# Gated attention's levels without the products of constants between them

## The reference

```python
def hybrid_layer(x, ...):
    proj = (rms_norm(x, pre_gain) * (1.0 + scale) + shift) @ w_in
    a_out = sliding_window_attention(aq, ak, av, sinks) * silu(ag)
    r_out = rms_norm(retention(rq, rk, rv)) * silu(rg)
    log_a = log_sigmoid(ga @ gla_gate_w + gla_gate_b) / 16.0
    g_out = rms_norm(gated_linear_attention(gq, gk, gv, log_a), gla_norm_gain) * silu(gg)
    y = concatenate([a_out, r_out, g_out]) @ w_out
    return x + gate * rms_norm(y, post_gain)

def gated_linear_attention(q, k, v, log_a):   # 4 heads, chunks of 64 tokens
    def step(state, inp):
        b = cumsum(gi, axis=2)
        rel = b[:, :, :, None, :] - b[:, :, None, :, :]
        decay = where(causal, exp(minimum(rel, 0.0)), 0.0)
        sc = einsum('bhid,bhijd,bhjd->bhij', qi, decay, ki)
        intra = einsum('bhij,bhjv->bhiv', sc, vi)
        inter = einsum('bhid,bhdv->bhiv', qi * exp(b), state)
        new_state = exp(b_last) * state + einsum('bhjd,bhjv->bhdv', ki * exp(b_last - b), vi)
        return new_state, intra + inter
```

## Time and profile before

| | |
|---|---|
| median of 3 runs | 2572.66 us (2561.11 to 2583.42) |
| profiled execution | 2573.33 us, its span 2571.6 us |
| mean granted TensorE clock | 0.962 |
| PE busy | 2359.1 us (92%) |
| DVE, POOL, ACT busy | 1318.0 (51%), 1064.4 (41%), 854.2 us (33%) |
| L245, all products of constants | 312 instructions, 78.2 us busy |

### The profile page before, as it was taken

One profiled execution on the slowest core, in us unless ns is written; L12 is line 12 of the kernel. 1 busy time (PEld: TensorE's weight loads), 2 busy tenths in 40 slices (PEclk: granted clock), 3 DMA queues, 4 the chain that ended last, 5 costly groups with the idle time before them and its releaser, 6 DMA issues.

```text
span 2571.6 us, 33845 instructions
## 1 busy us (share of the span) xinstructions
PE 2359.1 (92%) x13354; PEld 1980.2 (77%) x13354; DVE 1318.0 (51%) x2026; ACT 854.2 (33%) x1637; POOL 1064.4 (41%) x799
## 2 busy tenths in 40 slices
PE   4998898987989889888999999999798999999998
PEld 4777787776878656667998989999687677788886
DVE  6785636976559555477523513223678772110113
ACT  2124133224241666643221212112322883322222
POOL 4343346324362332323642433433652343645455
PEclk9998799989998999998999999999999999999999
DMA  8550024420224200023232313232261001223332
GB/s 283 174 165 1 19 81 148 147 83 1 75 70 146 54 2 1 9 79 127 82 99 86 110 58 115 82 95 94 78 196 43 8 2 49 82 92 98 98 99 74
DMA packets 147734, 218.99 MB, mean 85 GB/s; under 512 B 18484, under 2 KB 71124, under 8 KB 147448
## 3 DMA queue, kind: packets, MB, share of 16 engines
q1 hardware_dynamic: 147576, 216.82, 26.7%
HBM read 214.69 MB, written 2.10 MB: 84 GB/s over the span
## 4 chain that ended last, share of the span: by engine, by line
PE 55%; DVE 4%; ACT 3%; issue 2%; POOL 1%; ACTq 0%; DMA 0%; DVEq 0%; POOLq 0%; SPq 0%
PE ps L307 14%; PE ps L308 14%; PE ps L309 14%; PE ps L1008 5%; PE ps L1036 3%; PE ps L1058 2%; DVE mod_acc_aux L367 1%; PE ps L1305 1%; PE ps L1055 1%; POOL h_transposed L580 1%; PE ps L394 1%; PE ps L1300 1%; DVE x_tokens L867 1%; PE ps L592 0%; ACT att_probs_two L1098 0%
## 5 line engine op out<-in xcount | busy, mean ns | idle before, releaser
L296 POOL TENSOR_TENSOR w_lo<-w_raw,w_hi 128x1024 fp32r<-128x1024 f32 (+3 forms) x252 | 589.5, 2340 | 1002.6 <-ACT w_hi L289 1002.5
L289 ACT ACTIVATE w_hi<-w_raw 128x1024 fp32r<-128x1024 f32 (+3 forms) x252 | 255.7, 1016 | 1162.6 <-PE ps L309 981.1
L307 PE MATMUL ps<-w_hi,h_transposed 128*128 128x512 f32 (+3 forms) x1088 | 419.0, 385 | 57.2 <-POOL w_lo L296 30.7
L308 PE MATMUL ps<-w_lo,h_transposed 128*128 128x512 f32 (+3 forms) x1088 | 409.6, 376 | 0.0
L309 PE MATMUL ps<-w_hi,h_transposed 128*128 128x512 f32 (+3 forms) x1088 | 409.4, 376 | 0.0
L307 PE MATMUL ps<-h_transposed,w_hi 128*128 128x384 f32 (+1 forms) x1056 | 374.6, 355 | 8.3 <-POOL h_transposed L580 6.7
L308 PE MATMUL ps<-h_transposed,w_hi 128*128 128x384 f32 (+1 forms) x1056 | 373.9, 354 | 0.0
L309 PE MATMUL ps<-h_transposed,w_lo 128*128 128x384 f32 (+1 forms) x1056 | 373.8, 354 | 0.0
L367 DVE SCALAR_TENSOR_TENSOR mod_acc_aux<-w_raw,c_act,mod_acc_aux 128x512 f32<-128x512 f32 x280 | 279.1, 1021 | 45.0 <-DMA w_raw<-in_w_mod_dram 20.1
L307 PEld LDWEIGHTS ps<-w_hi,h_transposed 128*128 128x128 f32 x1088 | 214.4, 197 | 102.7 <-POOL w_lo L296 35.5
L1500 DVE TENSOR_TENSOR ffn_full<-ps,ffn_silu 128x768 f32<-128x768 f32 (+1 forms) x44 | 34.2, 819 | 427.5 <-PE ps L309 427.5
(11 more groups left out here) (318 smaller groups left out, 3527.5 us busy)
## 6 DMA issues: line engine op xcount, KB each, us to landing
w_raw<-in_ada_w_dram SPq DMA_DIRECT2D x96, 512.0 KB, 3.9
w_raw<-in_ffn_w_in_dram SPq DMA_DIRECT2D x88, 512.0 KB, 3.6
w_raw<-in_w_mod_dram SPq DMA_DIRECT2D x48, 512.0 KB, 4.6
w_raw<-in_ffn_w_out_dram SPq DMA_DIRECT2D x44, 512.0 KB, 3.5
w_raw<-in_w_in_dram SPq DMA_DIRECT2D x40, 512.0 KB, 4.5
w_raw<-in_w_out_dram SPq DMA_DIRECT2D x16, 512.0 KB, 4.3
w_raw<-in_od_w_in_dram SPq DMA_DIRECT2D x16, 512.0 KB, 4.3
mod_gain<-in_norm_g_dram SPq DMA_DIRECT2D x16, 256.0 KB, 4.3
```

The lines of the kernel that those rows point to most:

```text
L289: act.activation(w_hi[:, i % 2, 0:k * n], w_raw[:, u % 4, 0:k * n], ACT.Copy).then_inc(w_hi_ready.sem, 1)
L296: pool.tensor_tensor(w_lo[:, i % 2, 0:k * n], w_raw[:, u % 4, 0:k * n], w_hi[:, i % 2, 0:k * n].bitcast(F32), ALU.subtract).then_inc(w_lo_ ...
L307: pe.matmul(acc, left[0], right[0], start=start, stop=False)
L308: pe.matmul(acc, left[0], right[1], start=False, stop=False)
```

## The change

In `Memories.tensor` the products of constants before level 0 and between and behind the levels are taken out: 5 + 1 + 2 + 5 + 8 = 21 in each of the two layers, 42 in all. The 16 at the phase's end stay, as do those of other phases. Nothing else is changed; no wait and no signal hangs on the products.

```diff
                 self.retained(pe, 3)
-                keep_clock(pe, 5)
                 for l in range(len(LEVELS)):
                     self.level_scores(pe, l)
                     if l == 0:
...
                         self.retention_out(pe, 0)
-                        keep_clock(pe, 1)
                     if l == 1:
...
                     if l == 3:
                         self.retention_out(pe, 3)
-                        keep_clock(pe, 2)
-                    if l >= 4:
-                        keep_clock(pe, 5 if l == 4 else 8)
                 for t in range(XT):
                     self.gated_out(pe, t)
                 keep_clock(pe, 16)
```

## The result

The changed kernel took 2591.6 us (median of 9 runs, 2583.9 to 2597.0) and the kernel before, in the same jobs, 2573.2 us (9 runs). The ratio is 1.0077, with a 95% interval of 1.0053 to 1.0101: 0.8% slower, 0.4 us from the forecast of 2592 and within 1% as the likeliest case had it. The profiled execution has a span of 2589.8 us, 18.2 more than that of before, and a mean granted clock of 0.946 against 0.962. One of the twelve runs of experiment 5 (2786.9 us, mean clock 0.808) and one of experiment 6 (3864.1 us, 0.556) fell in a slow state at a low clock and are left out of what follows.

A forecast was written before the change was run, and what follows sets the result against it. TensorE at low clock bounds the levels, DVE from level 3's end to level 5's placing, TensorE the phase's end. First layer +5.25 and second +14.15 make +19.4 us on 2573.3: forecast 2592 us (chance 0.50), range 2571 to 2606.

The forecast's parts named there:

- The five before level 0, cost 0: Products before level 0: removal gives no time; a slower level 0 (1.99 for 1.13 us) hides in the 7.0 us gap.
- The product after the first output, 2.1 us gained: Single product ahead of level 1, on the path: removal saves 1.1 us in the first layer, 1.0 in the second.
- The second layer's levels at the low clock, +8.8 us: Without the product before level 1, the second layer's levels stay at low clock like the first's: +8.8 us, bounds 0 and 8.8.
- The outputs at the low clock, +5.1 us a layer: Four gated outputs after level 5 start at low clock and take 11.5 instead of 6.4 us; bounds 0 and 5.1.
- Rival 1: Clock returns by itself, in the gated outputs or the second layer's levels: +11.7 or +10.6 us, 2583 to 2585; chance 0.20.
- The closing sixteen, +1.25 us a layer: Sixteen products at the phase's end, on the path, spend 2.5 us at low clock, half lost; bounds 0.5 and 6.5.
- The late products, no time given back: Products after levels 3, 4 and 5 lie beside DVE's placing, so removing them gains 0.
- DVE's chain unchanged: DVE's steps from level 3's placing to level 5's stay at 12.6 us; a sign to check in the changed profile.
- Rival 2: Products are ballast; real work raises the clock after the first output: 2571 us, or 2562 if both layers rise; chance 0.10.
- rival 3: Low clock lasts through the closing sixteen, or next phase's transposes start low: 2 x 5.3 us more, 2603; chance 0.10.
- rival 4: Nothing seen, because before is often in the low case too and the later products' part is regained: 2576 to 2582; chance 0.10.
- the three times of before: 2561, 2573 and 2583 us could be both layers' levels at full clock, one, and none.

The follow-up runs named there:

- experiment 5: Kernel before without the five products ahead of level 0, in both layers: 2578.7 us, ratio 1.0014 to before.
- experiment 6: Kernel before with fourteen products in the wait behind level 0, without the one after the first output and the fifteen after levels 3 to 5: 2572.0 us, ratio 0.9996.
- experiment 1: Kernel before without the one product after the first retention output, in both layers: 2581.5 us, ratio 1.0008 to before.
- experiment 7: Changed kernel also without the closing sixteen products, so none in the phase: 2589.2 us, ratio 1.0061 to before.
- experiment 2: Kernel before without the fifteen products after levels 3, 4 and 5, in both layers: 2587.8 us, ratio 1.0047 to before.
- experiment 3: Kernel before with three products in place of the one after the first retention output: 2563.3 us, ratio 0.9948 to before.
- experiment 4: Kernel before with fourteen products in TensorE's wait behind level 0 and without the one after the first output: 2554.2 us, ratio 0.9908 to before.
- experiment 10: The kernel of experiment 4 run again, on the same chip as experiment 9: 2558.7 us, ratio 0.9934 to before.
- experiment 8: Kernel before with eight products before level 0, thirteen behind it, none after the first output, six instead of eight after level 5: 2558.1 us, ratio 0.9948.
- experiment 9: Kernel before with eight products before level 0, thirteen behind it, none after the first output, late ones unchanged: 2557.8 us, ratio 0.9937 to before.

## Why the prediction was right

**The five before level 0, cost 0:** right. The changed kernel's level 0 took 1.99 us, and experiment 5 shows the gap hiding it.

**The product after the first output, 2.1 us gained:** from the transposes' start to level 1's the layers took 3.47 and 3.46 us in place of 4.43 and 4.36, 1.9 us in all.

**The second layer's levels at the low clock, +8.8 us:** 31.34 - 22.66 = 8.7 us. That products in this place raise the clock, and not where the phase falls alone, is shown by the profiled layers: up before level 2 in none of six without one (changed kernel, experiments 1 and 7), in two of six with one (before and experiments 2 and 5), and in both with three (experiment 3). But the place counts as well, and one product failed more often than it worked.

**The outputs at the low clock, +5.1 us a layer:** 329.21 - 317.54 = 11.7 and 692.29 - 680.61 = 11.7 us against 6.4, so +5.3. Experiments 2 and 6 show it with levels 1 to 3 at the full clock in a layer. Rival 1, by which the outputs raise it themselves, fell: 0.50 over all 11.6 us.

**The closing sixteen, +1.25 us a layer:** 8.35 and 9.41 against 7.13 us, +1.2 and +2.3. The first is right; the second rose 4.6 us in (the sixteen begin at 692.29) and not 2.5. This term was too small in the second layer and in experiment 6 (+2.4 and +1.9). The price of 0.85 us for a product at the low clock was read from a pair in which the clock rose; it stands all the same, since a pair wholly at the low clock takes 2.02 us (experiment 1) and a single one 1.17.

**The late products, no time given back:** true of this pair of executions, in which all but the first layer's two after level 3 ran at the full clock. Where the single product fails more of them can run low and stand on the path, 2.3 and 3.4 us in experiment 1; the prediction had no such case.

**DVE's chain unchanged:** 304.95 to 317.39, 12.4 us, against 12.6. After the last output DVE needs 5.7 us (328.41 to 334.10) and not 5.3, which changes nothing, since the sixteen take over 7.

The phases' sum was forecast as +5.25 and +14.15 and measured as +5.4 and +15.4. The work elsewhere gave 2.6 back in this pair of executions, so the 19.4 of the sum met 18.2 in the profiled executions and 18.4 in the medians. That the forecast came within 0.4 us is luck: before's median alone moved from 2573.2 to 2577.9 us from job to job, and other work by up to 10 us from execution to execution.

The split of the sum is less sure than its size. It was worked out from one execution of before with one layer high. Over many runs, taking out the single product alone gave a ratio of 1.0008, where 8.8 - 2.1 us would be 1.0026, and the fifteen late ones alone 1.0047. So in the medians the outputs and the closing products seem to carry most of the loss, and the second layer's levels less than the 8.8 us they were given. How much less is open: 1.0026 is the very end of the first interval, and only one execution of before was profiled. The rule of the Trainium skill ("TensorE: Matmul & The Clock Gate", Part 1) that unbroken activity opens the gate did not hold for this work: 0.50 over 18.80 and 18.70 us of it in the changed kernel. Rival 2, which rests on the same idea, fell with it, and rival 3 with the closing products, in which the clock did return. Of rival 4 one half is likely true, that before is often in the low case (experiments 1 and 5), but the outputs' price was not regained.

**One remark of the prediction fell:** that the three times of before are the three cases of the two layers' levels. Its 26 runs in job one are spread over 2556 to 2588 without groups. The state of the levels is a part of the spread (with products in the wait it was 5 us over six runs in experiment 4 and 12 over eight in experiment 10, against 32 over 26 runs of before), and the work outside has the rest: 10 us in the last column of the table. The profiles place it in part. The first layer's phase begins anywhere from 256.15 us (experiment 2) to 261.90 (experiment 6) with nothing changed ahead of it, and its opening, up to level 0, takes 15.2 or 15.9 us.

## What to carry to other kernels

Before taking filler products out, look for what runs behind them at the full clock and ask what else would raise it: busy time in the profile does not answer that, the clock of a layer in which the same work ran without filler does. Filler costs nothing where TensorE waits for another engine anyway, and there it can hold the clock through a gap (here the wait of 7 us in each layer, for 0.5 to 0.9% of the kernel); the same product behind the gap stands on the path and may still fail. Filler at the low clock takes up to twice its time and can itself hold back the next step, as the six and eight after level 5 do. Where other work spreads by more than the effect, sum the stretch that was changed in each profile and compare those sums.

## What the runs showed of the hardware

In the changed kernel TensorE was busy without a break for 18.8 us of levels, updates and outputs at 0.50, and again for 11.6 us of gated outputs (128x256 state products on 64 columns and 128x64 products), and the clock did not rise in either layer; the closing products of 128x256 on all rows and columns raised it after 2.5 and 4.6 us. The clock was also lost without any long gap. Level 5 lasts 2.7 us behind DVE's placing and holds 32-row products with TensorE idle for some 0.4 us in all; the clock was 1.00 in it, and fell 0.8 to 0.9 us into the late products behind it, which were keeping TensorE fully busy, in the first layer of experiments 3, 4, 8, 9 and 10 (in experiment 4: 0.94 over 304.58 to 305.60, then 0.50 to 308.60; eight products took 5.41 in place of 3.72 us). In the second layer of experiments 8 and 9 it fell within level 5. But the same level 5 of 2.71 us kept the clock in the second layer of before and of experiments 3, 4 and 10. That such small products do not raise the clock was clear from before; that they do not surely keep it either was not expected, and what decides it was not tried.
